# A two-layer hybrid block: first modulation slabs loaded at once into empty buffers, last d_out slab computed branch product first

## The reference

```python
m = jax.nn.silu(c) @ w_mod[l] + b_mod[l]          # and mc from c_ctx
sh1, sc1, gt1, sh2, sc2, gt2 = jnp.split(m[:, None, :], 6, axis=-1)
h = _modulate(x, g_mix[l], sh1, sc1)              # rmsnorm(x, g) * (1 + sc) + sh
# from h @ w_in: short convolution (a), window attention (b), recurrence (c), 31-tap convolution (d)
ys = (a @ w_a_out, b @ w_b_out, c @ w_c_out, d @ w_d_out)
o = jnp.sum(sigmoid(gate_logits) * jnp.stack(ys), axis=branch) @ w_out
x = x + gt1 * o
x = x + gt2 * _swiglu(_modulate(x, g_ffn[l], sh2, sc2), w_ffn_in[l], w_ffn_out[l])
# after both layers: rmsnorm(x, g_final)
```

## Time and profile before

| | |
|---|---|
| median of 3 runs | 2291.26 us |
| the profiled execution, device time | 2297.54 us |
| its span | 2295.7 us |
| PE busy | 2110.1 us (92%), 11792 products |
| PE weight loads | 1744.3 us (76%) |
| DVE / ACT / POOL busy | 1202.5 (52%) / 915.5 (40%) / 780.6 (34%) us |
| loaded | 278.16 MB, mean 121 GB/s |
| granted clock of TensorE, mean | 0.964 of full speed |

### The profile page before, as it was taken

One profiled execution on the slowest core, in us unless ns is written; L12 is line 12 of the kernel. 1 busy time (PEld: TensorE's weight loads), 2 busy tenths in 40 slices (PEclk: granted clock), 3 DMA queues, 4 the chain that ended last, 5 costly groups with the idle time before them and its releaser, 6 DMA issues. The chain is left out here.

```text
span 2295.7 us, 31540 instructions
## 1 busy us (share of the span) xinstructions
PE 2110.1 (92%) x11792; PEld 1744.3 (76%) x11792; DVE 1202.5 (52%) x2042; ACT 915.5 (40%) x1420; POOL 780.6 (34%) x323
## 2 busy tenths in 40 slices
PE   5999998999989999898999999898899877899997
PEld 2677886778767777675777787677889867898997
DVE  3696204448889632134211212788545898545444
ACT  3696224432222332323222213499355322444433
POOL 1002442224433344321343344200534754233342
PEclk7999999999999999999999999999999988999998
DMA  7122221112212223554524322321442433344453
GB/s 293 55 74 91 75 93 70 49 50 106 92 74 74 74 73 128 221 204 169 219 87 182 134 87 100 118 88 64 146 143 105 167 113 109 130 157 151 170 182 129
DMA packets 38109, 278.16 MB, mean 121 GB/s; under 512 B 4352, under 2 KB 4352, under 8 KB 4736
## 3 DMA queue, kind: packets, MB, share of 16 engines
q1 hardware_dynamic: 38016, 276.87, 32.7%
HBM read 275.80 MB, written 1.05 MB: 121 GB/s over the span
## 5 line engine op out<-in xcount | busy, mean ns | idle before, releaser
L378 POOL TENSOR_TENSOR WL<-RAW,WH 128x1024 fp32r<-128x1024 f32 x319 | 780.4, 2464 | 1497.7 <-ACT WH L663 1497.7
L407 PE MATMUL PS<-HH,WH 128*128 128x512 f32 (+1 forms) x2272 | 821.1, 361 | 105.7 <-DVE ZL L1021 51.6
L407 PE MATMUL PS<-HL,WH 128*128 128x512 f32 (+1 forms) x2272 | 792.9, 349 | 0.0
L407 PE MATMUL PS<-HH,WL 128*128 128x512 f32 (+1 forms) x2272 | 791.8, 349 | 0.0
L663 ACT ACTIVATE WH<-RAW 128x1024 fp32r<-128x1024 f32 x416 | 417.3, 1052 | 739.2 <-PE PS L407 733.1
L407 PEld LDWEIGHTS PS<-HH,WH 128*128 128x128 f32 x2272 | 441.4, 194 | 190.9 <-issue 92.8
L407 PEld LDWEIGHTS PS<-HL,WH 128*128 128x128 f32 x2272 | 442.2, 195 | 57.3 <-issue 6.0
L407 PEld LDWEIGHTS PS<-HH,WL 128*128 128x128 f32 x2272 | 441.3, 194 | 56.5
L407 PE MATMUL PS<-ZH,WH 128*128 128x512 f32 (+1 forms) x992 | 341.9, 345 | 28.0 <-DVE ZL L1021 27.5
L407 PE MATMUL PS<-ZL,WH 128*128 128x512 f32 (+1 forms) x992 | 338.9, 342 | 0.0
L407 PE MATMUL PS<-ZH,WL 128*128 128x512 f32 (+1 forms) x992 | 338.7, 341 | 0.0
(11 more groups left out here) (134 smaller groups left out, 1549.2 us busy)
## 6 DMA issues: line engine op xcount, KB each, us to landing
RAW<-in_stream SPq DMA_DIRECT2D x208, 1024.0 KB, 4.8
CD<-in_modw SPq DMA_DIRECT2D x48, 1024.0 KB, 7.0
CD<-in_lruw SPq DMA_DIRECT2D x2, 2048.0 KB, 8.5
X<-in_xT SPq DMA_DIRECT2D x1, 2048.0 KB, 12.5
outT<-CD SPq DMA_DIRECT2D x1, 1024.0 KB, 3.8
PRM<-in_prm SPq DMA_DIRECT2D x1, 464.0 KB, 4.2
CST<-in_consts SPq DMA_DIRECT2D x1, 321.0 KB, 3.5
ROPE<-in_rope SPq DMA_DIRECT2D x1, 256.0 KB, 12.5
```

Source lines behind the costliest of these rows:

```text
L378: nc.gpsimd.tensor_tensor(WL[:, a:b], RAW[:, a:b], WH[:, a:b].bitcast(F32), ALU.subtract)\
L407: return nc.tensor.matmul(out, lhs, rhs, start=start, stop=stop)
```

## The change

In the opening SP loads `X` first, in two halves, then `CST` and `PRM`, and then issues modulation slabs 0 to 5 without a wait: 0 and 1 into `CD`, 2 and 3 into `G`, 4 into `TMP`, 5 into slot 1 of `RAW`. Stream slab 0 follows, modulation slabs 6 and 7 go to `CD` when slabs 0 and 1 were used, stream slab 1 when slab 5 was used, and `ROPE` last. PE sums the squares of `X` before the first modulation slab, and takes the columns of slab j-1 after the products of slab j. ACT rounds stream slab 0 between the copies of modulation slabs 5 and 6, and stream slab 1 after the first norm. POOL makes `WL` of slab 0 alone; DVE makes that of slab 1 after the norm. `G` is cleared in three narrow strips after modulation slabs 2 and 3 were used.

In `d_out` of both layers the last slab (n = 7) runs the branch product first and the gate logits second. During its second pass ACT writes rows 0 to 6 of `ZH` and DVE those of `ZL`. After it the sigmoid comes ahead of the rounding of the next slab. Row 7 follows when `S` has it. In layer 1 the half of `WL` that DVE makes for slab 1 of `w_out` comes after row 7 of `ZL`. To stay within the number of semaphores, some are shared by both layers (`both`, `Steps.base`).

```diff
 
+        MOD_HOMES = [CD[:, 0:SLAB], CD[:, SLAB:2 * SLAB], G[:, 0:SLAB], G[:, SLAB:2 * SLAB], TMP[:, 2 * NT:6 * NT],
+                     RAW[:, SLAB:2 * SLAB], CD[:, 0:SLAB], CD[:, SLAB:2 * SLAB]]
...
+        x_loaded, rope_loaded = [sem(f"x_loaded{j}") for j in range(2)], sem("rope_loaded")
+        first_loaded = [sem(f"first_loaded{j}") for j in range(2, 6)]
...
             sp.dma_start(CIN[:, :], cT).then_inc(in_loaded, 16)
+            for j in range(2):
+                part = slice(j * KC // 2 * NT, (j + 1) * KC // 2 * NT)
+                sp.dma_start(X[:, part], xT[:, part]).then_inc(x_loaded[j], 16)
             sp.dma_start(CST[:, :], consts).then_inc(par_loaded, 16)
             sp.dma_start(PRM[:, :], prm).then_inc(par_loaded, 16)
...
             for s in range(2):
                 load_mod(s, s)
-            sp.dma_start(X[:, :], xT).then_inc(x_loaded, 16)
-            sp.dma_start(ROPE[:, :], rope).then_inc(x_loaded, 16)
-            with sp.Fori(1, MOD_FIRST // 2) as i:
-                for s in range(2):
-                    sp.wait_ge(mod_used[s], i)
-                    load_mod(2 * i + s, s)
+            for j in range(2, 6):
+                sp.dma_start(MOD_HOMES[j], slab_of(modw, j)).then_inc(first_loaded[j - 2], 16)
+            load(0, 0)
             for s in range(2):
-                load(s, s)
+                sp.wait_ge(mod_used[s], 1)
+                load_mod(6 + s, s)
+            sp.wait_ge(mod_used[1], 3)
+            load(1, 1)
+            sp.dma_start(ROPE[:, :], rope).then_inc(rope_loaded, 16)
...
+            for h in range(2):
+                low(0, 0, h)
             after_norm = [pair_base(1, "c_in")] + [pair_base(l, "ff_in0") for l in range(DEPTH)]
-            runs = [(0, 1, 2)]
+            runs = [(0, 1, 0)]
...
-            def slab(m, s, ops, nk=KC, before=None, mods=(), ready=None):
+            def slab(m, s, ops, nk=KC, before=None, mods=(), ready=None, order=(0, 1)):
 
                 begin(m, s)
-                for t, (z, w) in enumerate(ops):
+                for j, t in enumerate(order):
+                    z, w = ops[t]
...
                     for slot, u in mods:
-                        (mod_products, mod_columns)[t](slot, u)
+                        (mod_products, mod_columns)[j](slot, u)
...
+            squares(0, "n1", NT)
             pe.wait_ge(silu_c, 1)
-            for s in range(2):
-                mod_products(s, 0)
-                mod_columns(s, 0)
-            squares(0, "n1", NT)
-            with pe.Fori(1, MOD_FIRST // 2) as i:
-                for s in range(2):
-                    mod_products(s, i)
-                    mod_columns(s, i)
+            for j in range(MOD_FIRST):
+                slot = j % 2
+                if 2 <= j < 6:
+                    pe.wait_ge(first_loaded[j - 2], 16)
+                else:
+                    pe.wait_ge(mod_loaded[slot], 16 if j < 2 else 32)
+                mod_rows_of(slot, MOD_HOMES[j])
+                if j > 0:
+                    mod_columns((j - 1) % 2, (j - 1) // 2)
+            mod_columns((MOD_FIRST - 1) % 2, (MOD_FIRST - 1) // 2)
...
-                stage(l, "d_out", [(H, W), (Z, W)], before=lambda k: pe.wait_ge(a["ln_l"].sem, k + 1))
+                stage(l, "d_out", [(H, W), (Z, W)], before=lambda k: pe.wait_ge(a["ln_l"].sem, k + 1), pairs=(0, 3))
+                b = pair_base(l, "d_out") + 3
+                use = MOD_IN[0, "d_out"][1] - 2 * MOD_IN[0, "d_out"][2] + 6
+                for s in range(2):
+                    slab(b, s, [(H, W), (Z, W)], mods=[(r, use + s) for r in range(2)] if l == 0 else [],
+                         order=(1, 0) if s else (0, 1))
                 pe.wait_ge(a["mod_v"].sem, a["mod_v"].at(0, "m3"))
...
+            for k in range(KC):
+                act.wait_ge(x_loaded[k // (KC // 2)], 16)
+                fn(row(S, k), row(X, k), ACT.Square).then_inc(L[0]["n1_a"].sem, 1)
             act.wait_ge(par_loaded, 32)
             decay(0)
-            for s in range(2):
-                mod_rows(s, 0)
-            act.wait_ge(x_loaded, 32)
-            norm_squares(0, "n1", NT, range(KC))
-            norm_root(0, "n1", 2)
-            with act.Fori(1, MOD_FIRST // 2) as i:
-                for s in range(2):
-                    mod_rows(s, i)
-            for s in range(2):
-                high(0, s)
+            act.wait_ge(eps_set, 3)
+            act.wait_ge(L[0]["n1_p"].sem, 1)
+            fn(tmp(0), bank(7), ACT.Sqrt, scale=1.0 / D, bias=EPSC).then_inc(L[0]["n1_a"].sem, 1)
+            for j in range(MOD_FIRST):
+                mod_rows(j % 2, j // 2)
+                if j == MOD_FIRST - 3:
+                    high(0, 0)
...
+                if l == 0:
+                    high(0, 1)
...
-                stage(l, "d_out", gate("do"))
-
-                read(act, l, "w_out")
-                for k in range(KC):
-                    out_of(act, l, "d_out", k)
-                    fn(row(ZH, k, W), row(S, k, W), ACT.Copy).then_inc(a["ws_a"].sem, 1)
+                stage(l, "d_out", gate("do"), some=(0, 3))
+                b = pair_base(l, "d_out") + 3
+                use = MOD_IN[0, "d_out"][1] - 2 * MOD_IN[0, "d_out"][2] + 6
+                for s in range(2):
+                    if l == 0:
+                        for r in range(2):
+                            mod_rows(r, use + s)
+                    if s:
+                        act.wait_ge(tile_done[s], 2 * b + 1)
+                        for k in range(KC - 1):
+                            out_of(act, l, "d_out", k)
+                            fn(row(ZH, k, W), row(S, k, W), ACT.Copy).then_inc(a["ws_a"].sem, 1)
+                    tiles(b, s)
+                    if s:
+                        gate("do")(6 + s, s, b)
+                        high(b + 1, s)
+                    else:
+                        high(b + 1, s)
+                        gate("do")(6 + s, s, b)
+                out_of(act, l, "d_out", KC - 1)
+                fn(row(ZH, KC - 1, W), row(S, KC - 1, W), ACT.Copy).then_inc(a["ws_a"].sem, 1)
...
-            V.memset(G[:, 0:GW * KC // 2], 0.0).then_inc(slab_out[0], 1)
-            V.memset(G[:, GW * KC // 2:GW * KC], 0.0).then_inc(slab_out[1], 1)
...
-                    dve.wait_ge(x_loaded, 32)
+                    for s in range(2):
+                        dve.wait_ge(x_loaded[s], 16)
                     inverse_root("n1", 2)
+                    for s in range(2):
+                        dve.wait_ge(mod_used[s], 2)
+                    rows = G[:, :].rearrange("p (k n) -> p k n", n=GW)
+                    V.memset(rows[:, :, 0:PAD], 0.0).then_inc(slab_out[0], 1)
+                    V.memset(rows[:, :, PAD + NX:PAD + NX + 2 * PAD], 0.0)
+                    V.memset(rows[:, :, GW - PAD:GW], 0.0).then_inc(slab_out[1], 1)
...
                 norm("n1", 0, 0, 2)
-                if l > 0:
-                    second_lows("c_in")
+                second_lows("c_in")
...
-                stage(l, "d_out", gated("do"))
-
+                stage(l, "d_out", gated("do"), some=(0, 3))
+                b = pair_base(l, "d_out") + 3
+                for s in range(2):
+                    if s:
+                        for k in range(KC - 1):
+                            dve.wait_ge(a["ws_a"].sem, k + 1)
+                            z_low(k, W, row(S, k, W)).then_inc(a["ws_v"].sem, 1)
+                    dve.wait_ge(tile_done[s], 2 * b + 2)
+                    gated("do")(6 + s, s, b)
+                    if l == DEPTH - 1 and s == 0:
+                        low(b + 1, s)
                 if l == 0:
                     modulation(16, 32, MOD_FIRST + 8, ("m3", None), 1, "g_ffn", 32)
-                for k in range(KC):
-                    dve.wait_ge(a["ws_a"].sem, k + 1)
-                    z_low(k, W, row(S, k, W)).then_inc(a["ws_v"].sem, 1)
+                dve.wait_ge(a["ws_a"].sem, KC)
+                z_low(KC - 1, W, row(S, KC - 1, W)).then_inc(a["ws_v"].sem, 1)
+                if l == DEPTH - 1:
+                    low(b + 1, 1)
```

More of the change, by code:

```diff
@@ L230, in st, with both @@
                 a[name] = Steps(sem(f"{name}_{l}"), names)
+            def both(name, names, turns):
+                a[name] = Steps(sem(name), names) if l == 0 else Steps(L[0][name].sem, names, turns * len(names.split()))
             st("lam_a", "abs exp")
@@ L251, in stage_sems @@
             st("ab_v", "e0 e1 p0 p1 l0")
[L252 to L256, removed]
+            for nm in ("co", "ao", "do"):
+                both(f"{nm}_a", "sg", KC)
+            st("bo_a", "sg")
+            both("ao_v", "t", KC)
+            both("do_v", "t", KC)
             st("bo_v", "s")
@@ L283, in stage_sems @@
             for f in range(len(FF_PARTS)):
-                st(f"fi{f}_a", "sg zh")
-                st(f"fi{f}_v", "p z")
-            return a
-        L = [stage_sems(l) for l in range(DEPTH)]
+                both(f"fi{f}_a", "sg zh", FF_PARTS[f])
```

(32 more changed lines are left out.)

15 lines of the change are left out of this document (8 added, 7 removed).

## The result

The changed kernel takes 2266.74 us, the median of 4 runs (2265.18 to 2274.93), against 2291.32 of the kernel before (4 runs, 2289.33 to 2298.77): ratio 0.989, interval 0.986 to 0.993, so 24.6 us less. The forecast was 2260.8 with a range of 2256 to 2268. The profiled execution took 2274.93 with a span of 2273.1, so 22.6 less than the one before (2297.54, 2295.7); the forecast for this pair was 30.5.

The account below looks back on a forecast made before the run. PE, busy nearly the whole span, was taken as the bound, so its idle and half-clock stretches count. Gains of 10.7 + 7.7 + 7.2 + 4.9 = 30.5 us took the median of 2291.26 to 2260.8, range 2256 to 2268.

Parts of the forecast that it names:

- What bounds the kernel: Whole kernel: PE is busy nearly throughout; its idle and half-clock stretches count, chiefly waits for `ZL` (79.1 us) and `HL` (35.3).
- The opening, up to the last modulation slab: Opening: loads queued ahead at 425 GB/s; slab 7's products end at 35.2 instead of 45.93; gain 10.7, bounds 9.4 to 12.0.
- From the last slab to the first pass: Up to `c_in`'s first pass: DVE no longer stands behind POOL, `lruw` takes back at most 0.4; gain 7.7, bounds 5.2 and 8.0.
- Layer 0: End of `d_out`, layer 0: PE idle 6.2 becomes 1.6, half-clock loss of 2.6 goes; gain 7.2, bounds 3.9 and 7.4.
- the clock's term: Layer 0, after the `d_out` gap: clock stays up after a 1.6 us gap, saving 2.6 of half-clock loss.
- a sign of being wrong: Listed as wrong: new PE stops in `c_in`, DMA share below 0.9 in the opening, or half clock after either `d_out` gap.
- Layer 1: End of `d_out`, layer 1: PE starts at once, stops before the eighth row for near 2.8; gain 4.9, bounds 1.8 and 5.3.
- Sum: Whole kernel: 10.7 + 7.7 + 7.2 + 4.9 = 30.5 us gained, giving 2260.8 against the median of 2291.26.
- the slow queue: Rival, opening: the long queue runs at some 360 to 390 GB/s; 2265.2 us; chance 14%.
- the choked one: Rival, opening: the deep queue falls under 207 GB/s and cancels all gains; at 190, 2296.7 us; chance 3%.
- `lruw` decides the start: Rival, start of `c_in`: `lruw` queues behind stream slab 1 and `ROPE`, costing +3.0; 2263.8 us; chance 6%.
- row 7: Rival, ends of `d_out`: row 7 replaces the wait as POOL holds DVE, in layer 1 the clock falls; 2264.6 us; chance 10%.

Follow-up runs that it names:

- the first trace: The changed kernel, first measurement, against the kernel before: median 2266.74 us, ratio 0.989; its profiled execution took 2274.93.
- the third: The changed kernel measured again, unaltered, on one chip with three variants, against a kernel before of 2289.50: 2268.58 us, ratio 0.989.
- the repeat: The changed kernel measured a second time, unaltered, beside variants holding parts of the change, against a kernel before of 2290.87: 2268.35 us, ratio 0.990.

## Why the prediction was right, point by point

- **What bounds the kernel**: right. The waits for `HL` and `ZL` are the ones that fell, at the opening and at the two ends of `d_out`.
- **The opening, up to the last modulation slab**: right in kind, the size off by 1.4. Products ended at 36.60 for 35.2, the gain 9.3 for 10.7, just under its lower bound of 9.4. The rate was 424 as taken; the sum went by bytes alone, and a slab has landed only when the last DMA engine has its part: one was a slab behind, so slab 6 came 1.8 late and slab 7 at 34.6 for 32.8. The half clock that the forecast priced was there too (1.93 for the last slab).
- **From the last slab to the first pass**: right. `AMP` and scalings in 1.9, PE's start on `lruw` 8.3 after the products (forecast 8.0), the second pass starts 16.4 after them (forecast for the end of the first 16.2). Gain 7.6 for 7.7. The hold by POOL is shown by putting it back (3.5 at the place).
- **Layer 0**: the stop came as forecast (1.58 for 1.6, released by `MOD`), 4.6 of gain. The failed step is "so short a gap leaves the clock up": PE ran at half clock for 3.4 us after it, and the clock's term was 1.0 instead of 2.6. Removing the stop gave 3.25. The prediction had named a half clock after this gap as a sign of being wrong, and it came, in all nine traces with this stop.
- **Layer 1**: PE started at once and stopped before row 7, for 2.58 (forecast 2.8). The forecast had 5.3 if the clock stays up and 2.7 if it falls, and took 4.9 with half of the order at row 7 left open. `S` was held. The clock fell in the first trace and in the third, and the gain is 3.8 and 3.9; in the repeat it stayed up, and the gain is 5.2. So both branches occur, and a fall costs 1.4, not 2.6.
- **Sum**: the step that failed is that the four gains add. 26.3 was won locally and 22.6 left in the profiled pair, 24.6 in the medians. The forecast held every other gap's cost fixed, though the traces have gaps of 2.5 to 3.0 that end at either clock, and a DVE-bound stage whose length depends on POOL's phase. That the time fell inside the range is in part luck: 2266.74 is above the forecast's own range (2257 to 2264), and the two later measurements of the change, 2268.35 and 2268.58, are above 2268. The forecast also took 0.2% as what a measurement can tell; the intervals here reach 0.1 to 0.4% to either side.
- **Rivals**: the slow queue is refuted (424 and 421 GB/s over 30 us), the choked one too; `lruw` decides the start, as forecast, and came 0.3 later than that; row 7 took part of the gain in layer 1. No rival named half clock elsewhere or the stage of `a_cu` and `a_b`, which moved the end by more than any of them.

## What to carry to other kernels

A stop of TensorE can cost more than its length: taking out one of 1.58 us gave 3.25. In a kernel with many stops near the edge, count the local gains and then expect some us back or on top from half-clock stretches elsewhere, and compare variants at several common gaps, not at the end alone, and by more than one trace of each. Before sending work to GpSimd, look at which VectorE instructions beside it have all their operands in SBUF: those waited here for whole instructions of the other.

## What the runs showed of the hardware

- TensorE fell to half clock after the stop of 1.58 us in all nine traces that have it (clock 0.50 over 955 to 958), while before one of 2.88 left it at full (1.00 over 220.3 to 223.9). After the stop of 2.6 before row 7 it fell in four traces and stayed up in four, and the change itself is among both (0.71 and 1.00). The length of a stop alone doesn't tell, nor does the kernel.
- One core loaded at 421 to 424 GB/s for 30 us with some ten MiB issued ahead. The limit of some 358 GB/s that the Trainium skill gives in "DMA: Bandwidth & Descriptors" (Specifications) is passed by 18%; its page "HBM Reference" (Specifications (TRN2)) puts that figure down to two cores that load at once and has about 425 for a core alone, and this trace agrees with the latter.
- A transfer of 1 MiB counts as landed with the last of 16 DMA engines. With slabs 6 and 7 one engine's part came up to 2.3 us behind the others' (DMA share 0.06 from 32.3 to 34.6, with nothing issued behind slab 7).
- VectorE's instructions over SBUF (0.41 to 0.48 us for 256 columns) took up to 2.6 while GpSimd ran, as `TENSOR_TENSOR` and as `SCALAR_TENSOR_TENSOR`; 256 with an operand in PSUM never took over 0.49. So it is by the Trainium skill too ("SBUF — State Buffer", Who interferes with whom: two SBUF inputs contend with a GpSimd instruction that reads SBUF; at most one doesn't, outside the modes that use both port pairs; and the order of issue decides who blocks). `TENSOR_SCALAR` with one tensor from SBUF (`TMP<-PADA,PRM`) was held as well, for 2.55 instead of 0.45. What was not expected is how much hangs on it far from the edit: 40 to 48 us of a stage of 137 to 146 are in the groups that can be held.
